# A two-layer transformer kernel: the recurrence's gates as pairs of 64-row matmuls

## The reference, cut to what matters

```
u_pad = pad(u); xc = conv_b + sum_k u_pad[:, k:k+s] * conv_w[k]        # 4 taps
xb = xc.reshape(b, s, 12, 64)
r = sigmoid(einsum('bsgi,gij->bsgj', xb, w_r) + b_r)                   # gate 1, one 64x64 matrix per block
i = sigmoid(einsum('bsgi,gij->bsgj', xb, w_i) + b_i)                   # gate 2, the same form
log_a = -8 * softplus(-lam) * r;  a = exp(log_a)
gated_x = sqrt(-expm1(2 * log_a)) * (i * xc)
h_t = a_t * h_(t-1) + gated_x_t                                        # scan over the tokens
```

## Time and profile before

| what | value |
|---|---|
| median of three runs | 3132.32 us |
| the profiled execution, its own time | 3131.1 us |
| its span, first to last instruction | 3129.0 us |
| PE busy | 3066.4 us, 98% of the span |
| ACT busy, DVE busy | 1329.6 us (42%), 1791.4 us (57%) |
| granted clock of PE | 0.996 of full speed |
| the recurrence's six strips | about 2854 to 3033 us of the span |

### The profile page before, as it was taken

One profiled execution on the slowest core, in us unless ns is written; L12 is line 12 of the kernel. 1 busy time (PEld: TensorE's weight loads), 2 busy tenths in 40 slices (PEclk: granted clock), 3 DMA queues, 4 the chain that ended last, 5 costly groups with the idle time before them and its releaser, 6 DMA issues.

```text
span 3129.0 us, 50323 instructions
## 1 busy us (share of the span) xinstructions
PE 3066.4 (98%) x18600; PEld 2608.8 (83%) x18600; DVE 1791.4 (57%) x3573; ACT 1329.6 (42%) x2637; POOL 664.3 (21%) x886
## 2 busy tenths in 40 slices
PE   7999999999999999999999999998999999999999
PEld 7988888999999888888788888888977777787777
DVE  6657674353344322345888887876353666753675
ACT  5446565454445221232333333454433555522552
POOL 3423334453542000001111111001101011032240
PEclk9999999999999999999999999999999999999999
DMA  5110011011111321122233225643100000221012
GB/s 204 37 48 18 21 35 51 28 62 44 56 59 46 103 78 51 45 95 97 72 109 109 102 101 204 196 151 140 46 28 22 16 28 15 108 72 67 28 61 101
DMA packets 77412, 231.27 MB, mean 74 GB/s; under 512 B 17712, under 2 KB 21936, under 8 KB 65648
## 3 DMA queue, kind: packets, MB, share of 16 engines
q1 hardware_dynamic: 77168, 228.05, 20.8%
HBM read 183.92 MB, written 43.84 MB: 73 GB/s over the span
## 4 chain that ended last, share of the span: by engine, by line
PE 90%; DVE 6%; ACT 2%; issue 1%; DMA 1%; SPq 0%; POOL 0%; DVEq 0%; ACTq 0%; POOLq 0%
PE ps L2546 71%; PE ps L2589 7%; PE ps L2597 3%; PE ps L2553 2%; PE ps L2604 2%; PE ps L2620 2%; PE ps L2612 1%; PE ps L2623 1%; PE ps L2640 1%; DVE wlo L2815 0%; DVE hlo L2892 0%; ACT hhi L2660 0%; ACT whi L2650 0%; DVE qk L2923 0%; DMA fa2r<-scratch_fs 0%
## 5 line engine op out<-in xcount | busy, mean ns | idle before, releaser
L2546 PE MATMUL ps<-whi,hhi 128*128 128x256 f32 (+2 forms) x1920 | 580.5, 302 | 3.0 <-DVE hlo L2892 1.7
L2546 PE MATMUL ps<-whi,hlo 128*128 128x256 f32 (+2 forms) x1920 | 563.7, 294 | 0.0
L2546 PE MATMUL ps<-wlo,hhi 128*128 128x256 f32 (+2 forms) x1920 | 563.4, 293 | 0.0
L2546 PEld LDWEIGHTS ps<-whi,hhi 128*128 128x128 f32 x1920 | 368.2, 192 | 12.8 <-issue 5.1
L2546 PEld LDWEIGHTS ps<-wlo,hhi 128*128 128x128 f32 x1920 | 368.8, 192 | 7.4 <-issue 0.2
L2546 PEld LDWEIGHTS ps<-whi,hlo 128*128 128x128 f32 x1920 | 368.2, 192 | 7.7
L2546 PE MATMUL ps<-hhi,whi 128*128 128x512 f32 x864 | 342.3, 396 | 0.0
L2546 PE MATMUL ps<-hhi,wlo 128*128 128x512 f32 x864 | 337.0, 390 | 0.0
L2546 PE MATMUL ps<-hlo,whi 128*128 128x512 f32 x864 | 336.3, 389 | 0.0
L3154 POOL TENSOR_SCALAR stats<-stats 128x2 f32<-128x2 f32 (+2 forms) x230 | 59.3, 258 | 1194.1 <-ACT xsf L2654 509.1
L3143 POOL CAST whi<-raw 128x512 fp32r<-128x512 f32 (+4 forms) x180 | 113.7, 631 | 865.8 <-PE ps L2546 856.1
(11 more groups left out here) (616 smaller groups left out, 6996.6 us busy)
## 6 DMA issues: line engine op xcount, KB each, us to landing
raw<-in_W SPq DMA_DIRECT2D x61, 1024.0 KB, 4.8
scratch_fs<-fo SPq DMA_DIRECT2D x77, 256.0 KB, 2.0
raw<-in_W SPq DMA_DIRECT2D x24, 768.0 KB, 4.3
wd<-in_WD SPq DMA_DIRECT2D x44, 256.0 KB, 3.5
wf0b<-in_WF SPq DMA_DIRECT2D x10, 1024.0 KB, 5.3
wf1b<-in_WF SPq DMA_DIRECT2D x10, 1024.0 KB, 5.2
scratch_x<-x SPq DMA_DIRECT2D x16, 512.0 KB, 3.3
orw<-scratch_outs SPq DMA_DIRECT2D x6, 1024.0 KB, 5.8
```

The costliest lines, as they stand in the source:

```text
L2546: x = e.matmul(r.out, a, b, start=(r.start and m == 0), stop=(r.stop and m == n - 1), skip_group_check=r.joined)
```

## The change

The matrices of both gates are laid out anew. (The line numbers of the kernel after it differ from those before by up to 6.) `lw` has one matrix of 128 rows and 128 columns for each strip, in place of two. Rows 0 to 63 hold the first block's two matrices side by side, `[w_r | w_i]`, and rows 64 to 127 hold the second block's, `[w_i | w_r]`. For each half of the tokens PE multiplies rows 0 to 63 into one bank and rows 64 to 127 into a second bank. So the first bank holds rg of block 0 over ig of block 0, and the second ig of block 1 over rg of block 1. ACT then reads each bank in two pieces of 64 rows, and writes each to its rows of `rg` or `ig`. The bias of gate `ig` is rotated by 64 rows in the input to match. The number of matmul instructions stays at 24 (two for each half of a strip, each of 64 rows in place of 128), and the tanh instructions go from 24 to 48. A record now holds two banks. PE waits for both before the first of its two matmuls.

```
-        lw = rest("lw", [6, 2, 128], F, 64 * KB + 512)
+        lw = rest("lw", [6, 128], F, 64 * KB + 512)
...
-            for gi, (dst, bias) in enumerate(((rg, ex), (ig, zq))):
-                for hf in range(2):
-                    r = Rec()
-                    r.cut = slice(hf * 512, hf * 512 + 512)
-                    r.place, r.w, r.conv, r.free = DB.take(), lw[:, s, gi, :], L.conv[hf], prev
-                    r.dst, r.bias = dst[:, r.cut], bias[:, s:s + 1]
-                    emit("lru_gate", r)
-                    L.gates = r.place.read
-                    m = r.place.full
+            for hf in range(2):
+                r = Rec()
+                r.s, r.cut = s, slice(hf * 512, hf * 512 + 512)
+                r.places, r.conv, r.free = [DB.take(), DB.take()], L.conv[hf], prev
+                emit("lru_gate", r)
+                L.gates = r.places[1].read
+                m = r.places[1].full
                 next(att_steps, None)
...
                 elif kind == "lru_gate":
-                    w.wait_ge(*r.place.before)
+                    for place in r.places:
+                        w.wait_ge(*place.before)
                     w.wait_ge(*r.conv)
                     w.wait_ge(*t_lw)
-                    e.matmul(r.place.ps[:, :], r.w, xc[:, r.cut], start=True, stop=True).then_inc(r.place.full[0], 1)
+                    for place, rows in zip(r.places, (slice(0, 64), slice(64, 128))):
+                        x = e.matmul(place.ps[:, :], lw[rows, r.s, :], xc[rows, r.cut], start=True, stop=True)
+                        x.then_inc(place.full[0], 1)
...
                 elif kind == "lru_gate":
-                    w.wait_ge(*w.last)
-                    w.wait_ge(*r.place.full)
                     w.wait_each(r.free)
                     w.wait_ge(*t_lm)
-                    e.activation(r.dst, r.place.ps[:, :], ACT.Tanh, scale=0.5, bias=r.bias).then_inc(w.sig(r.place.read), 1)
+                    up_, down_ = slice(0, 64), slice(64, 128)
+                    for place, parts in zip(r.places, (((rg, ex, up_, up_), (ig, zq, down_, up_)),
+                                                       ((ig, zq, up_, down_), (rg, ex, down_, down_)))):
+                        w.wait_ge(*place.full)
+                        for x, (dst, bias, src, to) in enumerate(parts):
+                            w.wait_ge(*w.last)
+                            a = e.activation(dst[to, r.cut], place.ps[src, :], ACT.Tanh, scale=0.5, bias=bias[src, r.s:r.s + 1])
+                            a.then_inc(w.sig(place.read) if x else w.inner(), 1)
```

More of the change, by code:

```diff
@@ L2388, in build @@
                                       for i, n in enumerate(("xc", "rg", "ig", "av", "tv", "hs", "gg"))]
-        lw = rest("lw", [6, 2, 128], F, 64 * KB + 512)
-        t_lw = load("lruw", lw[:, :, :, :], d["lruw"], free1, ln_tok[7])
+        lw = rest("lw", [6, 128], F, 64 * KB + 512)
+        t_lw = load("lruw", lw[:, :, :], d["lruw"], free1, ln_tok[7])
         t_kv1b = load("kv1b", kv[0][:, :, :, :], d["kv1"], t_kv1, o2_last)
@@ L3222 @@
         "conv_w": a["lru_conv_w_2"][0].reshape(4, 6, 128).transpose(2, 1, 0).reshape(128, 24),
-        "conv_b": feat(a["lru_conv_b_2"]), "b_r": feat(a["lru_b_rgate_2"]), "b_i": feat(a["lru_b_igate_2"]),
+        "conv_b": feat(a["lru_conv_b_2"]), "b_r": feat(a["lru_b_rgate_2"]), "b_i": np.roll(feat(a["lru_b_igate_2"]), 64, axis=0),
         "lru_lam": feat(a["lru_lambda_2"]),
@@ L3226 @@
     }
-    lruw = np.zeros((128, 6, 2, 128), np.float32)
-    for gi, name in enumerate(("lru_w_rgate_2", "lru_w_igate_2")):
-        for blk in range(12):
-            o = 64 * (blk % 2)
-            lruw[o:o + 64, blk // 2, gi, o:o + 64] = a[name][0, blk]
+    both = [a[name][0].reshape(6, 2, 64, 64) for name in ("lru_w_rgate_2", "lru_w_igate_2")]
+    lruw = np.stack([np.concatenate([both[x][:, x], both[1 - x][:, x]], axis=2) for x in range(2)], axis=1)
+    lruw = lruw.reshape(6, 128, 128).transpose(1, 0, 2)
     tab_a, tab_b, tab_m = tables()
```

## The result

The kernel after the change takes 3144.69 us (median of five runs, 3140.65 to 3145.52), against 3132.25 us for the kernel before in five runs beside it. The ratio is 1.0039 with a 95% interval of 1.0027 to 1.0050, so it is slower by 8.5 to 15.7 us, 12.2 us in the middle. The forecast was 3140.5 us, 8 us more than before. Its direction and most of its size came true. Its account of the last 4 us did not: the measured median lies inside the whole range (3130 to 3145.5), but just above the forecast's own range (3136.5 to 3144).

The account below looks back on a forecast made before the run. PE was taken as the bound, with a loop over ACT and DVE that has little room. Matmuls gave -8.6 us and idle time +17.0, so 3131.1 + 8.4 = 3139.5 profiled, 3140.5 as forecast; own range 3136.5 to 3144, whole range 3130 to 3145.5.

Parts of the forecast that it names:

- The added tanh: Gates on ACT: 24 more tanh at 0.72 us each, 17 us in all, 2.88 a strip.
- rival B: Loop over ACT and DVE: gaps of 4.00 and 7.04 us mostly take up ACT's lateness; 3131 us, chance 0.15.
- The matmuls: Gate pairs on PE: about 1.05 us for four instructions against 1.81, saving 8.6 us in all.
- rival D: Gate pairs: the two halves don't overlap at 512 columns, 0.86 us more a pair; 3143.5 us, chance 0.03.
- Rival A: Gate matmuls on PE: their 8.6 us gain comes through whole; 3123.7 us, chance 0.08.
- The 3123.7 us: Whole kernel: the time by the skill's "Theoretical Speedup" alone, up to 2x for 64 rows.
- The idle time: PE, from strip 0's last transposes to after strip 5: 17.0 us of added idle time.
- The clock: PE's matmuls: counted at full clock in the sum, with a lower clock after waits priced only as a rival.
- Rival C: Strips 1 and 3: waits of about 3 us lower PE's clock, up to 3.0 us lost; 3143.5 us, chance 0.08.
- signs of being wrong: Tanh under 0.5, strip 1's second pair before 2908, no lateness at its `av`, or clock under 0.95 in strips 1 to 4.
- The end: In and after strip 5: `av` is 8.4 us late, and PE takes over the full 8.4.
- two waits for `hlo`: End of the recurrence: PE's waits of 0.23 and 0.50 us for `hlo` stay.

Follow-up runs that it names:

- e2: The kernel before, with each gate tanh cut into two pieces of 64 rows (48 tanh), matmuls as they were: 3141.28 us, ratio 1.0029.
- e7: The changed kernel with one 128-row tanh a bank, and only 64 of 512 columns read from each pair's second bank; output wrong: 3125.97 us, ratio 0.9982.
- e1: The changed kernel with its paired matmuls, but one 128-row tanh a bank (24 in all); output partly wrong: 3128.71 us, ratio 0.9992.
- e9: The changed kernel with filler matmuls during PE's wait for the second pair's second bank, three in strips 1 and 3, one in strip 4: 3140.54 us, ratio 1.0028.
- e10: The change in strip 5 alone, the other five strips as in the kernel before: 3134.19 us, ratio 1.0006.
- e5: The changed kernel with longer filler matmuls during PE's wait, five in strips 1 and 3, three in strip 4: 3145.68 us, ratio 1.0045.
- e12: The change in strips 0 to 4, strip 5 as in the kernel before: 3139.83 us, ratio 1.0027.
- e6: The changed kernel, with PE waiting for a pair's two banks one at a time: 3142.55 us, ratio 1.0039.
- e4: The changed kernel with four 64x64 quadrants a bank pair, 24 tanh, and DVE's product putting ig's exchanged halves in place: 3129.37 us, ratio 0.9991.

## Why the prediction came out as it did

**The added tanh: right.** The forecast had ACT late at `av` by 1.7, 3.9, 4.3, 6.5, 7.9 and 8.4 us in strips 0 to 5. With the tanh alone (e2) it is late by 1.5, 3.8, 4.0, 6.2, 7.5 and 8.1. So the loop from ACT over DVE's `tv`, scan and maxima back to ACT has no slack that counts, and rival B (the lateness is taken up) is out. In the changed kernel the gap of DVE ahead of `tv` grew from 4.00 to 5.32, as a wait inside a loop does, and did not shrink as a reserve would:

```profile
2889.92 1.23 DVE L3130 SCALAR_TENSOR_TENSOR tv<-av,tv 128x1024 f32<-128x1024 f32 x1 [5.32 <-ACT tv L2810]
```

**The matmuls: price right, place wrong.** A pair costs 0.96 to 1.06 us to the next start, as forecast, and rival D (the halves don't overlap) is out. Rival A needs the gain to come through whole, and not even e7, with ACT relieved, has all of it. (The 3123.7 us that the prediction sets beside a factor of two holds its own 8.6 us; half of 24 matmuls of 0.86 us would be 10.3.) The Trainium skill, "TensorEngine Tiling (Array Packing)", section "PSUM Bottleneck", warns that tiling leaves the reading of PSUM as it was. The trace agrees, with a factor of 1.7 to 1.9 (1.81 against 1.06 and 0.96) on under 1% of PE's time (24 matmuls of 0.86 us, 21 of 3066): 4.2 us of e1's saving went into waits for banks.

**The idle time: close.** 17.0 us were forecast. The trace has 15.7 (15.5 more than before): 2.92 and 2.92 at the second pairs of strips 1 and 3 (3.0 and 3.5 by the forecast), 2.08 in strip 4, 1.64 in strip 2.

**The clock: the step that failed.** The sum of the forecast has every matmul at full clock. Rival C priced two drops at up to 3.0 us, but as a case beside the forecast, with a chance of 0.08. It belonged into the sum: its own condition, waits of about 3 us in strips 1 and 3, was what the forecast itself had worked out. And a clock under 0.95 in strips 1 to 4 was one of the prediction's own signs of being wrong; it was 0.83 over ten us in two of them. The lateness at `av` in the changed kernel parts from e2's by 1.1 in strip 1 and 0.9 in strip 4, where the pair ran slowly, and by 0.9 more in strip 5, which PE reaches late by the slow matmuls behind strip 4's pair. e9, without these two drops, is less late than the changed kernel by 0.7 us from strip 1 on and by 2.2 in strip 5. That is 2.5 of the 3.4 us of stretch between the changed kernel and e2. The other 0.9 is not shown to be the clock's, since e2 and e9 both have 0.83 behind strip 5. The places were not quite C's: strips 1 and 4 and the end, not 1 and 3.

**The end: right amount, wrong reason.** The forecast kept the two waits for `hlo` and had PE take over the lateness there. In the trace the next layer's first matmuls wait 2.11 and 0.53 us for the tanh of strip 5 to empty their banks, and those two `hlo` waits are gone. The lower clock there (0.94 and 0.89) cost little. The matmuls behind the wait ran 1.4 us longer than in e10, where the same two waits left the clock at 1.00. But e10's PE then waited 0.76 us for `hlo`, and from the matmul that waited 2.1 us to the 29th further matmul of its kind (`whi,hhi`), 21.69 us in e10 (3038.98 to 3060.67), the changed kernel takes 22.06 (3047.73 to 3069.79), only 0.4 us more. The amount, 2.9 from strip 5, stood for e10 as 2.8.

**What stays open.** By PE's account 15.5 - 8.6 = 6.9 us, and slower matmuls have to give the other 4.9. From the second pair's start to the next strip's first matmul (line 2544) PE took 4.13 us in strip 1 (2912.71 to 2916.84) against 2.75 in e9 (2911.85 to 2914.60), and 3.39 against 1.95 in strip 4. So the pair and the scores or values behind it ran slowly together, 1.4 us in each. With the 1.4 behind strip 5 that is 4.2 of the 4.9; 0.7 is not placed. Why strip 4, with a wait of 2.08 us, lost the clock and strip 3, with 2.92, kept it, was not tested. Nor was why the end kept 1.00 in e5 and e10.

## What to carry to other kernels

A saving on the busiest engine is worth what its suppliers let it use: here 8.6 us of matmuls gave 3.4 with ACT unchanged, and nothing with ACT 17 us longer. An engine at 42% of the span can have no room where it counts; look for the packed piece and for a loop that leaves the engine and comes back. If an instruction's price doesn't depend on its rows, don't cut it by rows: let another engine, or the layout of the product, put the rows in place. And when a forecast makes new waits, put the clock behind them into the sum.

## What the runs showed of the hardware

- The length of a wait did not decide the clock. After 2.92 us in strip 1 the granted clock was 0.83 and the pair lasted 2.08 us; after the same 2.92 in strip 3 it was 1.00 and the pair lasted 1.13. e12 repeated both. The waits of 2.1 and 0.5 us behind strip 5 were followed by 1.00 in e5 and e10 and by 0.83 in e6 and e9. The Trainium skill, "TensorE: Matmul & The Clock Gate", Part 1, has idling as the cause; e9 agrees, where work in the wait kept the clock at 1.00.
- Four quadrants of 64x64 with 512 columns into two banks last 1.09 us, as long as two halves of 64x128 (1.13).
- A tanh and a DVE product of 64 rows cost what 128 rows cost: 0.683 against 0.687, and in e4's strip 1 two products of 64 rows took 2.47 us, and one of 128 rows in e1's strip 1 took 1.22.
